# Final norm of a mixture-of-experts step: bulk tiles in nine borrowed buffers, roots by groups, a ScalarE square root for the last rows

## What is computed

```
hid = silu(xe @ w_gate[e]) * (xe @ w_up[e])          # xe: the rows that expert e chose
ye  = (hid @ w_down[e]) * gate                       # added back to the rows, times g_m
x   = x + g_m * sum over e of ye
y   = x * rsqrt(mean(x * x) + 1e-6) * final_norm_g   # y_prompt (128 rows), y_sample (2048 rows)
```

## Time and profile before

| | us |
|---|---|
| median of 3 runs | 2360.68 |
| lowest, highest | 2358.61, 2364.14 |
| the profiled execution | 2361.86 |
| its span | 2359.5 |

### The profile page before, as it was taken

One profiled execution on the slowest core, in us unless ns is written; L12 is line 12 of the kernel. 1 busy time (PEld: TensorE's weight loads), 2 busy tenths in 40 slices (PEclk: granted clock), 3 DMA queues, 4 the chain that ended last, 5 costly groups with the idle time before them and its releaser, 6 DMA issues.

```text
span 2359.5 us, 39435 instructions
## 1 busy us (share of the span) xinstructions
PE 2181.6 (92%) x15547; PEld 2013.9 (85%) x15547; DVE 1359.2 (58%) x2106; ACT 991.3 (42%) x1714; POOL 261.7 (11%) x402
## 2 busy tenths in 40 slices
PE   4999999996799999828999999999999999999985
PEld 2878888885588888618999999999999999999984
DVE  2656542407477777485565555656564556565565
ACT  3642221224355555214444444434454444444552
POOL 0000000000011111110000000000000000000474
PEclk8999999998699999858999999999999999999998
DMA  8533443138344444115565566566566656566783
GB/s 287 177 124 133 137 148 116 57 122 249 94 142 131 131 138 148 63 70 180 189 205 177 181 192 215 164 191 191 200 179 190 196 187 199 168 198 196 239 294 143
DMA packets 320060, 397.62 MB, mean 169 GB/s; under 512 B 11598, under 2 KB 273246, under 8 KB 317918
## 3 DMA queue, kind: packets, MB, share of 16 engines
q1 hardware_dynamic: 288990, 287.21, 37.6%
q0 software_dynamic: 24624, 96.48, 13.2%
q10 hardware_dynamic: 6352, 12.65, 1.5%
HBM read 320.22 MB, written 76.09 MB: 168 GB/s over the span
## 4 chain that ended last, share of the span: by engine, by line
PE 49%; POOL 3%; issue 1%; DMA 1%; DVE 1%; ACT 1%; POOLq 0%; ACTq 0%; DVEq 0%
PE experts_ps_r L2407 45%; PE experts_ps_x L2387 1%; PE experts_ps_o L2397 1%; POOL experts_fst L2241 1%; POOL experts_fst L2242 1%; POOL experts_fst L2238 1%; PE experts_ps_i L2301 0%; DMA experts_xf<-x 0%; POOL experts_fst L2239 0%; DMA out_y_sample<-experts_onehot 0%; ACT experts_whi L2488 0%; DMA experts_xg<-normed,experts_idx 0%; ACT experts_junk L2521 0%; POOL out_y_sample L2226 0%; PE experts_ps_x L2363 0%
## 5 line engine op out<-in xcount | busy, mean ns | idle before, releaser
L2623 DVE TENSOR_TENSOR experts_wlo<-experts_raw,experts_whi 128x2048 fp32r<-128x2048 f32 x192 | 440.1, 2292 | 385.5 <-ACT experts_whi L2488 385.4
L2407 PE MATMUL experts_ps_r<-experts_xhi,experts_whi 128*128 128x272 f32 x2048 | 603.5, 295 | 8.8 <-DVE experts_xlo L2676 5.5
L2407 PE MATMUL experts_ps_r<-experts_xhi,experts_wlo 128*128 128x272 f32 x2048 | 593.9, 290 | 0.0
L2407 PE MATMUL experts_ps_r<-experts_xlo,experts_whi 128*128 128x272 f32 x2048 | 590.7, 288 | 0.0
L2407 PEld LDWEIGHTS experts_ps_r<-experts_xhi,experts_whi 128*128 128x128 f32 x2048 | 387.0, 189 | 9.2 <-DVE experts_xlo L2676 5.8
L2407 PEld LDWEIGHTS experts_ps_r<-experts_xlo,experts_whi 128*128 128x128 f32 x2048 | 387.7, 189 | 0.0
L2407 PEld LDWEIGHTS experts_ps_r<-experts_xhi,experts_wlo 128*128 128x128 f32 x2048 | 386.5, 189 | 0.0
L2488 ACT ACTIVATE experts_whi<-experts_raw 128x2048 fp32r<-128x2048 f32 x192 | 366.2, 1907 | 13.8 <-DMA experts_raw<-in_w_gate 13.0
L2407 PE MATMUL experts_ps_r<-experts_hhi,experts_whi 128*128 128x272 f32 x1024 | 302.6, 296 | 3.1 <-DVE experts_hlo L2807 3.0
L2407 PE MATMUL experts_ps_r<-experts_hhi,experts_wlo 128*128 128x272 f32 x1024 | 296.9, 290 | 0.0
L2407 PE MATMUL experts_ps_r<-experts_hlo,experts_whi 128*128 128x272 f32 x1024 | 295.4, 288 | 0.0
(11 more groups left out here) (478 smaller groups left out, 3242.8 us busy)
## 6 DMA issues: line engine op xcount, KB each, us to landing
experts_raw<-in_w_gate SPq DMA_DIRECT2D x64, 1024.0 KB, 4.8
experts_raw<-in_w_up SPq DMA_DIRECT2D x64, 1024.0 KB, 4.8
experts_raw<-in_w_down SPq DMA_DIRECT2D x64, 1024.0 KB, 5.0
shared_whalf<-in_w_ada SPq DMA_DIRECT2D x16, 1024.0 KB, 5.2
ssd_mz<-mixed SPq DMA_DIRECT2D x17, 768.0 KB, 7.7
mixed<-front_acc POOLq DMA_DIRECT2D x9, 1024.0 KB, 4.2
resid<-early_xin POOLq DMA_DIRECT2D x17, 512.0 KB, 3.4
ssd_xs<-resid SPq DMA_DIRECT2D x17, 512.0 KB, 4.0
```

The costliest lines, as they stand in the source:

```text
L2407: mm = pe.matmul(dst, w[:, c % RING, kk, cols], r[:, kk, :], start=(kk == 0 and q == 0), stop=(kk == KD - 1 and q == 2))
L2623: dve.tensor_tensor(wlo[:, c % RING, :, :], raw[:, c % RAW, :, :], whi[:, c % RING, :, :].bitcast(F32), ALU.subtract).then_inc(wlo_done, 1)
```

## The change

- Nine buffers instead of five. The rows of `yo` and `xg` are lent: tiles 0 and 1 live in `yo`, 2 in the spare row, 3 and 4 in `onehot`, 5 and 6 in `xg`, 7 and 8 in `xf`; tiles 9 to 15 reuse the homes of tiles 2 to 8. Each home has one semaphore for loads and stores.
- `rows_out` of expert 14 waits on VectorE, before it writes either half of `yo`, for the store of tile 0 or 1.
- GpSimd finds roots for groups of 5, 2, 2, 3, 2 and 2 tiles at once, in fourteen instructions each instead of eight per tile. It uses tensor_tensor, where one-column pointer operands were used.
- The steps of the squares and scalings are moved, and the order of GpSimd's loads, groups and stores is new. Both gathers stand behind the last group, in front of the last two stores; the gather into `xg` waits for the stores of tiles 12 and 13.
- The last rows, and the rows of expert 14, get their root from a ScalarE square root and a VectorE reciprocal.
- On VectorE `add_before` moves from `dt` 1 to 3, the first `shared_rows` from 3 to 4, the second from 5 to 6, behind `scale_before`.

```diff
+FIRST = 9
+HOME = tuple(range(FIRST)) + tuple(range(2, FIRST))
+ROOTS = ((0, 5), (5, 7), (7, 9), (9, 12), (12, 14), (14, 16))
-SQUARES = {(NE - 2, 6): (0,), (NE - 2, 7): (1,), (NE - 2, 8): (2,), (NE - 2, 15): (3,), (LAST, 0): (4,), (LAST, 1): (5,),
-           (LAST, 2): (6,), (LAST, 3): (7,), (LAST, 4): (8, 9), (LAST, 5): (10,), (LAST, 6): (11,), (LAST, 7): (12,),
-           (LAST, 8): (13,), (LAST, 9): (14,), (LAST, 11): (15,)}
-SCALES = {(NE - 2, 9): (0,), (NE - 2, 12): (1,), (NE - 2, 13): (2,), (LAST, 0): (3,), (LAST, 1): (4,), (LAST, 2): (5,),
-          (LAST, 3): (6,), (LAST, 4): (7,), (LAST, 5): (8, 9), (LAST, 6): (10,), (LAST, 7): (11,), (LAST, 8): (12,),
-          (LAST, 9): (13,), (LAST, 10): (14,), (LAST, 12): (15,)}
+SQUARES = {(NE - 2, 6): (0, 1), (NE - 2, 7): (2,), (NE - 2, 8): (3,), (NE - 2, 9): (4,), (NE - 2, 11): (5,), (NE - 2, 12): (6,),
+           (NE - 2, 15): (7,), (LAST, 0): (8,), (LAST, 1): (9,), (LAST, 2): (10, 11), (LAST, 4): (12, 13), (LAST, 6): (14, 15)}
+SCALES = {(NE - 2, 12): (0, 1), (NE - 2, 13): (2, 3), (NE - 2, 14): (4,), (LAST, 0): (5,), (LAST, 1): (6,), (LAST, 2): (7,),
+          (LAST, 3): (8,), (LAST, 4): (9,), (LAST, 5): (10, 11), (LAST, 6): (12, 13), (LAST, 8): (14,), (LAST, 9): (15,)}
...
-        fbuf = [g.spare, hot_room[:, 0, :], hot_room[:, 1, :], xf_rows[:, 0, :], xf_rows[:, 1, :]]
+        room = [yo[:, 0, :], yo[:, 1, :], g.spare, hot_room[:, 0, :], hot_room[:, 1, :], xg[:, 0, :], xg[:, 1, :],
+                xf_rows[:, 0, :], xf_rows[:, 1, :]]
...
+        def bulk_wait(eng, i, stored):
+            eng.wait_ge(bulk_moved[HOME[i]], 32 * (i // FIRST) + (32 if stored else 16))
...
             def load(i):
-                if 1 <= i < 3:
-                    pool.wait_ge(comp_done, NE)
-                elif 3 <= i < 5:
-                    pool.wait_ge(xlo_done, NE)
-                elif i >= 5:
-                    pool.wait_ge(bulk_stored[i % NF], 16 * (i // NF))
+                if i >= FIRST:
+                    bulk_wait(pool, i - FIRST + 2, True)
...
-            def find_root(i):
-                ssq, half, root, more = (fst[:, i, n:n + 1] for n in range(4))
-                pool.wait_ge(sq_done, i + 1)
+            def find_roots(q):
+                lo, hi = ROOTS[q]
+                ssq, half, root, more = (fst[:, lo:hi, n] for n in range(4))
+                pool.wait_ge(sq_done, hi)
                 root_step(pool.tensor_scalar(half, ssq, 0.5 / D, 0.5 * EPS, ALU.mult, ALU.add))
                 root_step(pool.tensor_scalar(root.bitcast(I32), half.bitcast(I32), -0.5, SEED, ALU.mult, ALU.add))
                 for _ in range(3):
-                    root_step(pool.tensor_scalar(more, root, root, half, ALU.mult, ALU.mult))
-                    root_step(pool.tensor_scalar(root, more, 1.5, root, ALU.subtract, ALU.mult))
+                    root_step(pool.tensor_tensor(more, root, root, ALU.mult))
+                    root_step(pool.tensor_tensor(more, more, half, ALU.mult))
+                    root_step(pool.tensor_scalar(more, more, -1.0, 1.5, ALU.mult, ALU.add))
+                    root_step(pool.tensor_tensor(root, more, root, ALU.mult))
...
             pool.wait_ge(added, 32 * (NE - 2))
             for i in range(3):
                 load(i)
+            pool.wait_ge(comp_done, NE)
+            load(3)
+            load(4)
+            pool.wait_ge(xin_done, NE * 8)
+            load(5)
             load(6)
+            find_roots(0)
+            pool.wait_ge(xlo_done, NE)
+            load(7)
+            load(8)
+            find_roots(1)
+            for i in range(5):
                 store(i)
+            load(9)
+            find_roots(2)
+            load(10)
+            load(11)
+            store(5)
+            load(12)
+            store(6)
+            find_roots(3)
+            load(13)
+            store(7)
+            store(8)
+            load(14)
+            find_roots(4)
+            store(9)
+            load(15)
+            for i in range(10, 14):
+                store(i)
+            find_roots(5)
+            pool.wait_ge(ctx_chain, C_SAVED)
+            for a in range(2):
+                bulk_wait(pool, 12 + a, True)
+                pool.indirect_dma_start(xg[:, a, :], None, io["x2"], bass.IndirectOffsetOnAxis(idx[2][:, a:a + 1], 0)
+                                        ).then_inc(gathered, 16)
...
+            store(14)
+            store(15)
...
+            def spread_of(at, n):
+                act.activation(fst[:, at:at + n, 1], fst[:, at:at + n, 0], ACT.Sqrt, bias=g.eps[:, 0:1], scale=1.0 / D
+                               ).then_inc(std_done, 1)
...
+            act.wait_ge(ctx_chain, C_SSQ)
+            spread_of(F_LAST, 3)
...
-            def rows_out(e, f):
+            def rows_out(e, f, last=False):
                 a, half = f // 2, f % 2
                 cols = slice(512 * half, 512 * half + 512)
                 dve.wait_ge(outt_done, e * 4 + (f + 1))
+                if last and half == 0:
+                    bulk_wait(dve, a, True)
...
-                step(dve.tensor_scalar(half, fst[:, at:at + len(rows), 0], 0.5 / D, 0.5 * EPS, ALU.mult, ALU.add))
-                step(dve.tensor_scalar(root.bitcast(I32), half.bitcast(I32), -0.5, SEED, ALU.mult, ALU.add))
-                for _ in range(3):
-                    step(dve.tensor_tensor(more, root, root, ALU.mult))
-                    step(dve.tensor_tensor(more, more, half, ALU.mult))
-                    step(dve.scalar_tensor_tensor(root, more, 1.5, root, ALU.subtract, ALU.mult))
+                dve.wait_ge(std_done, stage)
+                std, root = (fst[:, at:at + len(rows), n] for n in (1, 2))
+                step(dve.reciprocal(root, std))
...
-                        if left == 0 and dt == 1:
+                        if left == 0 and dt == 3:
                             add_before()
-                        if left == 0 and dt == 3:
+                        if left == 0 and dt == 4:
                             shared_rows(0)
                             shared_rows(1)
-                        if left == 0 and dt == 5:
+                        if left == 0 and dt == 6:
+                            scale_before()
                             shared_rows(2)
                             shared_rows(3)
-                        if left == 0 and dt == 6:
-                            scale_before()
```

More of the change, by code:

```diff
@@ L2247, in _ @@
             loops(body, pool)
-            n_lat = NT - 1
-            uses = [len(range(b, n_lat, NF)) for b in range(NF)]
             pool.wait_ge(added, 32 * (NE - 2))
@@ L2719, in context_in, with scale_rows @@
                      C_SCALED + kk // 2 + 1)
[L2721 to L2731 removed]
+            def scale_rows(rows, at, stage):
+                dve.wait_ge(std_done, stage)
+                std, root = (fst[:, at:at + len(rows), n] for n in (1, 2))
+                step(dve.reciprocal(root, std))
                 for n, ap in enumerate(rows):
@@ L2785, in scale_before @@
             def scale_before():
-                scale_rows([xg[:, a, :] for a in range(2)], F_BEFORE, F_BEFORE + 2)
+                scale_rows([xg[:, a, :] for a in range(2)], F_BEFORE, 1)
             def finish():
```

81 lines of the change are left out of this document (32 added, 49 removed).

## The result

| | before | after |
|---|---|---|
| median of 8 runs each, side by side | 2364.05 us (2358.61 to 2367.01) | 2372.55 us (2369.07 to 2378.86) |
| ratio to before | 1 | 1.0042, 95% interval 1.0029 to 1.0055 |
| profiled execution, span | 2361.86, 2359.5 us | 2373.48, 2371.8 us |
| GpSimd busy over the span | 261.7 us | 237.3 us |

The account below looks back on a forecast made before the run. GpSimd's queue (load, root, store) was taken to set the pace beside expert 15. Idle times and clock falls + 11.1, tail - 1.65: + 9.4 on 2361.86 is 2371.3, median 2370 us; range 2364 to 2378, 8 in 10 2350 to 2381.

Parts of the forecast that it names:

- The first group: GpSimd's first group of roots, behind five squares and held by VectorE's subtractions, ends at about 2233.2.
- the added wait: `rows_out` of expert 14 on VectorE waits for tile 0's landed store, issued at 2248.1: TensorE idle 3.9 us (was 1.23).
- The squares that wait for loads: ScalarE's squares of tiles 9, 13 and 15 wait for loads: TensorE idle 0.2, 7.9 and 7.3 us.
- The two squares: Two ScalarE squares at feed-forward tile 6 of expert 14 instead of one: TensorE idle 0.45 -> 1.55 us.
- The clock: TensorE's clock falls behind long idle times, 1.4 us each: three falls after, two before.
- The root steps: GpSimd's root steps: 6 x 4.1 = 24 us of work where it was 48; queue order, not work, ends last.
- The block rule: A GpSimd step waits out VectorE instructions with two SBUF inputs, back-to-back ones as a block: 0.29 us becomes 4.43.
- block of six: VectorE's four scalings of tiles 0 to 3, a split and tile 4's scaling, end to end: 8.2 us from 2233.2.
- GpSimd gets in between: Rival, chance 0.12: a waiting GpSimd step enters at each VectorE boundary, five more steps through, 1.5 us; 2366 us.
- The tail: Eleven VectorE steps at the end, 2.2 us, become a ScalarE square root and reciprocal, 0.56: gain 1.65 us.
- The sum: Idle times 20.9 plus three clock falls, 25.1 us against 14.0: + 11.1, less 1.65, + 9.4.

Follow-up runs that it names:

- after with two steps: After, in its own queue order, with the twelve Newton steps of each group of roots left out: 2351.61 us, ratio 0.9959.
- kernel with both orders: After with stores 0 to 4 ahead of the second group of roots and load 15 ahead of the fifth: 2357.67 us, ratio 0.9977.
- stores first: After with stores 0 to 4 ahead of the second group of roots in GpSimd's queue: 2362.70 us, ratio 1.0001.
- spread kernel: The kernel with both orders, with squares mostly one to a place and groups of roots and scalings rearranged: 2361.64 us, ratio 0.9997.
- early gathers: The spread kernel with one gather right behind the fifth group of roots, the other ahead of the sixth, three scalings moved: 2355.45 us, ratio 0.9969.

## Why the prediction was right, and where it was not

The forecast was 2370 us and slower; 2372.55 was measured. The forecast starts from before's first three runs (median 2360.68); over the eight beside after, before's median is 2364.05. The fairer measure is the difference: + 9.3 us of median said, 8.5 by the medians and 9.9 by the ratio measured. The mechanism is the one forecast, and the closeness of the number owes something to luck. In its steps:

*The first group and the added wait: right.* The group ended at 2233.34 (said: 2233.2), store 0 went out at 2246.98 (2248.1), `rows_out` began at 2252.12 (2251.7), TensorE stood 3.21 us (3.9). Two of its terms were off and cancelled: the second group ended 1.1 us sooner (below), and the landing took 5.1 us instead of 3.6. The clock did not fall behind this idle time, as I had it; it fell behind the 2.86 us.

*The squares that wait for loads: right in kind, shared out wrongly.* I had 0.2 + 7.9 + 7.3 = 15.4 us for what was 0.19 + 2.86 + 3.72 + 9.27 = 16.0. The 2.86 us I had missed: squares 10 and 11 stand in one place, behind a split that square 9's wait had made late, square 11 waits 0.79 us more for its load, and the weight block behind them is wanted already at feed-forward tile 4. The pair alone is not enough: after with two steps has it, no square waits there, and TensorE has no idle time at that place. The 2.86 us and the slow clock behind them brought TensorE that much later to the block at tile 6, so 7.9 became 3.72. The last one was sized by a landing of 4.5 us for load 15; it took 8.9, from 2298.95 to 2307.86, with stores 9 to 13 issued around it. The kernel with both orders confirms the mechanism: load 15 ahead of the roots, 9.53 to 2.62 us.

*The two squares: right.* 1.69 us for 1.55, and 0.46 when they are apart.

*The clock: under-sized, and one fall elsewhere.* Three falls as said, but one of them stands behind the 2.86 us that the forecast did not have, in place of the one at `rows_out`: the count was right by luck. They cost 6.6 us instead of 3 x 1.4 = 4.2. Two were the expensive ones: 29 products at 0.212 us behind the 2.86 us, and 22 at 0.225 us behind the 9.27 us.

*The root steps: unit and saving right, the hold-ups left out, their worth wrong.* A free step takes 0.20 us, 0.28 begin to begin, as taken. I put the bulk's root work at 48 us before and 24 after, undisturbed; with the hold-ups the busy time of its lines is 31.0 + 19.2 + 12.9 + 7.1 = 70 us in before, and some 46 us in after. The difference is 24 us either way. But that GpSimd's order is what ends last, and not its work, is half the truth. The order alone is worth 10 us of after (stores first) and 15 with load 15, both with all steps kept. Yet the Newton steps are worth 20 us in after's order and 14.5 in before's. In after the order hurts because a group is long, and the length hurts because something urgent is queued behind it; either cure works. In before the urgent thing is the root itself: ten scalings wait for one.

*The block rule: half right.* GpSimd's timeline under the scalings of tiles 0 to 4 (VectorE: four scalings from 2233.38, the split from 2238.16, a scaling from 2240.36 to 2241.64):

```profile
2234.87 1.04 POOL L2243 TENSOR_SCALAR experts_fst<-experts_fst 128x2 f32<-128x2 f32 x1
2235.99 1.11 POOL L2244 TENSOR_SCALAR experts_fst<-experts_fst 128x2 int32<-128x2 int32 x1
2237.19 3.31 POOL L2246 TENSOR_TENSOR experts_fst<-experts_fst 128x2 f32<-128x2 f32 x1
2240.58 1.12 POOL L2247 TENSOR_TENSOR experts_fst<-experts_fst 128x2 f32<-128x2 f32 x1
```

One step gets in at most boundaries, and 3.31 us lie across a scaling and the split behind it. So four steps came through beneath the block of six where I had three; five more ran in a gap of 1.25 us ahead of the next split, which I had put end to end with the block. The rival "GpSimd gets in between" described this place better than the forecast did; the group ended 1.1 us sooner, not the 1.5 it claimed, and the gain went into the longer landing. The first group's steps were not held across the two subtractions at 2224.60 and 2226.81 either (2.25 and 2.12 us, one each), where before has 4.43 over such a pair. The Trainium skill, "SBUF — State Buffer", Who interferes with whom, says that who issues first decides; the 1.04, 1.11 and 1.12 us agree with that, the 3.31 does not. Why one boundary lets a step in and another doesn't, no run here tells.

*The tail: right.* 0.82 us from the sum to the scalings instead of 2.41: 1.59 for the 1.65 said. One table load, 1.28 us at 2340.16, off the path; none in the tail.

```profile
2339.95 0.19 ACT L2543 ACTIVATION_READ_ACCUMULATOR experts_junk<-experts_xg 128x1 f32 x1
2340.16 1.28 ACT L2558 ACT_TABLE_LOAD   x1
2341.45 0.30 ACT L2558 ACTIVATE experts_fst<-experts_fst,kept_eps 128x2 f32<-128x2 f32 x1
2356.62 0.30 ACT L2558 ACTIVATE experts_fst<-experts_fst,kept_eps 128x3 f32<-128x3 f32 x1 [0.23 <-DVE experts_fst L2821]
...
2356.42 0.17 DVE L2821 TENSOR_TENSOR experts_fst<-experts_fst 128x3 f32<-128x3 f32 x1 [0.79 <-ACT experts_junk L2543]
2357.24 3.68 DVE L2758 SCALAR_TENSOR_TENSOR experts_raw<-experts_raw,experts_fst,kept_logits 128x1024 f32<-128x1024 f32 x3
```

The Trainium skill, "ScalarE: Activation LUTs", What ACT_TABLE_LOAD costs, adds a drain to the load. No drain is seen here: ScalarE works up to 2340.14, the load begins 0.02 us later and the square root 1.29 us after the load does.

The sum, then: + 9.4 said for the profiled execution, + 11.6 measured (2373.48 - 2361.86). The idle times agree to 0.1 us (9.65 said, 9.75 measured) through misses that cancelled, which is luck; what stayed short is the clock term, by 1.9 us (3.3 for 1.4).

## What to carry to other kernels

In a queue that carries both arithmetic and transfers, ask of each transfer what is computed ahead of it and who waits for its landing: batching the arithmetic saves instructions and delays every transfer behind the batch, and two swaps in such a queue were worth 15 us here with every instruction kept. An engine can be the bound at 70% busy, when its work stands in a chain with waits on both sides: a quarter fewer steps gave nearly the whole gain. And when a chain is shortened, look at once for what ends next, for it takes over: here a gather stood behind the last group of roots, and when it was moved ahead of the group, a lent buffer's landed store held it to the same date.

## What the runs showed of the hardware that I had not expected

The clock stayed at 1.00 behind an idle time of 3.21 us and fell behind one of 2.86 us that came 20 us later; the length of an idle time alone did not tell which. In after with two steps it stayed at 1.00 behind 2.53 us, in before it fell to 0.66 behind 2.57.

Transfers of 512 KB from GpSimd's queue took longer where more of them went out together. The median from issue to landing of the stores out of `onehot` between 2235 and 2310 us is 4.3 to 6.3 us in the kernel before and its four versions, where they mostly go out one at a time, and 6.7 to 8.8 us in after and its eight. The same stores of tiles 9 to 13 landed in 2.9 to 4.2 us in the spread kernel, where they went out between 2288 and 2297 us, and in 6.5 to some 8 us in the one with the early gathers, where they went out within 3 us behind a gather. No run changes the number in flight alone, so the crowd as the cause is likely and not shown.

A switch of ScalarE's table cost the 1.28 us of the load and no more, although ScalarE worked up to it.
